# The first RMS root from the token rows of x, x loaded ahead of the modulation weights

## The reference

```python
mod = split(silu(c) @ ada_w + ada_b, 6)                  # six vectors of 1024 channels
h = x * rsqrt(mean(x * x, axis=-1) + 1e-6) * g_pre       # first root: one number per token
a = h * (1 + mod[1]) + mod[0]                            # a scale and a shift per channel
b_gate, c_gate, v = split(a @ sc_w_in, 3)
y = (b_gate * conv3(c_gate * v)) @ sc_w_out
x = x + mod[2] * rmsnorm(y, g_post)                      # its own norm follows: the second root of x
```

## Time and profile before

| | us |
|---|---|
| median of 3 runs | 1722.91 |
| lowest and highest run | 1722.45, 1723.51 |
| the profiled execution | 1723.58 |
| its span, first to last instruction | 1721.8 |
| PE busy in it | 1697.1 (99%) |
| DVE busy | 1096.6 (64%) |
| ACT busy | 699.0 (41%) |

### The profile page before, as it was taken

The page is one execution under the profiler, slowest core; times in us unless marked ns, Lnnn a source line. Parts: engine busy times, 40 slices in busy tenths (PEclk is TensorE's granted clock), DMA queues, the critical chain, the costliest instruction groups (busy, mean ns, idle before and its releaser), DMA issues.

```text
span 1721.8 us, 21514 instructions
## 1 busy us (share of the span) xinstructions
PE 1697.1 (99%) x7685; PEld 1374.9 (80%) x7685; DVE 1096.6 (64%) x1663; ACT 699.0 (41%) x1021; POOL 159.3 (9%) x145
## 2 busy tenths in 40 slices
PE   8999999999999999999999999999999999999999
PEld 7888868888888789788888888877656888888888
DVE  6799885353534685645663663669998666366364
ACT  4322353232323345844432432446676443243242
POOL 1000400000000040000000000005892000000000
PEclk9999999999999999999999999999999999999999
DMA  9576314323333132002222222232210323223222
GB/s 295 178 243 221 125 57 137 98 98 98 116 98 98 49 99 93 31 26 98 98 98 98 97 98 89 81 99 74 74 49 28 120 97 99 85 94 112 75 85 86
DMA packets 182338, 176.22 MB, mean 102 GB/s; under 512 B 3304, under 2 KB 181740, under 8 KB 182268
## 3 DMA queue, kind: packets, MB, share of 16 engines
q1 hardware_dynamic: 182268, 175.29, 31.8%
HBM read 173.15 MB, written 2.10 MB: 102 GB/s over the span
## 4 chain that ended last, share of the span: by engine, by line
PE 87%; DVE 5%; POOL 4%; issue 2%; ACT 1%; DMA 1%; POOLq 0%; SPq 0%; DVEq 0%; ACTq 0%
PE PSUM L1582 23%; PE PSUM L1583 23%; PE PSUM L1584 23%; POOL CP L537 3%; DVE PSUM L1514 1%; PE PSUM L1947 1%; PE PSUM L1945 1%; PE PSUM L1946 1%; PE PSUM L1920 1%; PE PSUM L1900 1%; PE PSUM L1672 1%; PE PSUM L1614 1%; PE PSUM L1616 1%; PE PSUM L1979 1%; PE PSUM L1980 1%
## 5 line engine op out<-in xcount | busy, mean ns | idle before, releaser
L577 ACT ACTIVATE WH<-RAW 128x1024 fp32r<-128x1024 f32 x274 | 281.5, 1052 | 726.6 <-PE PSUM L1584 684.5
L1582 PE MATMUL PSUM<-XH,WH 128*128 128x512 f32 x1152 | 449.5, 390 | 0.0
L1583 PE MATMUL PSUM<-XL,WH 128*128 128x512 f32 x1152 | 448.2, 389 | 0.0
L1584 PE MATMUL PSUM<-XH,WL 128*128 128x512 f32 x1152 | 448.2, 389 | 0.0
L977 DVE TENSOR_TENSOR WL<-RAW,WH 128x1024 fp32r<-128x1024 f32 x274 | 343.6, 1276 | 8.1 <-ACT WH L577 8.0
L1582 PEld LDWEIGHTS PSUM<-XH,WH 128*128 128x128 f32 x1152 | 216.3, 188 | 45.7 <-issue 0.7
L1583 PEld LDWEIGHTS PSUM<-XL,WH 128*128 128x128 f32 x1152 | 216.3, 188 | 45.4 <-issue 0.7
L1584 PEld LDWEIGHTS PSUM<-XH,WL 128*128 128x128 f32 x1152 | 216.3, 188 | 44.8
L1582 PE MATMUL PSUM<-HH,WH 128*128 128x512 f32 x644 | 251.3, 390 | 0.4
L1584 PE MATMUL PSUM<-HH,WL 128*128 128x512 f32 x644 | 250.6, 389 | 0.0
L1583 PE MATMUL PSUM<-HL,WH 128*128 128x512 f32 x644 | 250.6, 389 | 0.0
(11 more groups left out here) (347 smaller groups left out, 2000.7 us busy)
## 6 DMA issues: line engine op xcount, KB each, us to landing
RAW<-in_ffn_w_up SPq DMA_DIRECT2D x44, 1024.0 KB, 5.0
ARAW<-in_ada_w SPq DMA_DIRECT2D x24, 1024.0 KB, 5.3
RAW<-in_mlp_w_in SPq DMA_DIRECT2D x16, 1024.0 KB, 5.3
RAW<-in_mlp_w_out SPq DMA_DIRECT2D x16, 1024.0 KB, 4.9
RAW<-in_ffn_w_down SPq DMA_DIRECT2D x16, 1024.0 KB, 5.1
RAW<-in_sc_w_in SPq DMA_DIRECT2D x9, 1024.0 KB, 5.2
RAW<-in_even_w_in SPq DMA_DIRECT2D x8, 1024.0 KB, 5.6
RAW<-in_odd_w_pw SPq DMA_DIRECT2D x16, 512.0 KB, 4.7
```

The lines of the kernel that those rows point to most:

```text
L577: act.activation(WH[:, j, a:b, :], RAW[:, j, a:b, :], ACT.Copy).then_inc(s_hi, 1)
L1582: pe.matmul(o, wh, mh[:, k, :], start=(k == 0), stop=False)
L1583: pe.matmul(o, wh, ml[:, k, :], start=False, stop=False)
L1584: mm = pe.matmul(o, wl, mh[:, k, :], start=False, stop=(k == kn - 1))
```

## The change

x is loaded in four blocks of 128 tokens, ahead of all modulation weights. ACT squares each block of rows as it lands, with the sum over the channels accumulated per token, takes ln and exp of the 128x4 sums, and writes the roots on four diagonals of 128x128; PE multiplies these by ones, which puts the root of every token on all partitions in `ST_BANK`, where `scaled_x` reads it. The squares and additions of the chunks on ACT, POOL and DVE and their two sums on PE are gone. PE transposes block by block, DVE copies half a block at a time. The scale column of chunk 0 is made by PE alone (`first_scale`, 8 steps), so that `mod_unit(4, P)` covers chunk 1 alone. The shift column of chunk 0 has a semaphore of its own, and the four last shift steps of stage 0 come behind chunk 0's products of the first unit. DVE makes the columns of the chunks one by one; `mod_unit(5)` stands ahead of chunk 1's subtraction. On PE the fillers at the start are 16 rather than 26, the shift products of stage 1 and its scale columns are put elsewhere between the products. Since the bank now holds the root, ACT turns it back into the mean square (Ln, Exp with -2) before unit 12, and DVE's last addition for the second root multiplies by 1024.

```diff
-    return 8 * (stat - (stat > ST_X1))
+    return 8 * (stat - (stat > ST_X0) - (stat > ST_X1))
...
+        SCALE_BANK, SHIFT_BANK = 3, 6
...
                 a = (4 + i, i)[part]
                 if i == 1:
-                    sp.wait_ge(s_xt, DC)
-                elif i >= 2:
-                    sp.wait_ge((s_ad, s_ap)[part], i - 1)
+                    sp.wait_ge(s_xt, 2 * TB)
+                    sp.wait_ge(s_xq, TB)
+                elif i == 2:
+                    sp.wait_ge((s_ac, s_ap)[part], 1)
+                elif i == 3:
+                    sp.wait_ge((s_ad, s_ap)[part], 2)
...
+                                 ).then_inc(s_raw0[i] if i else s_raw00[u], 16)
...
+            for b in range(TB):
+                sp.dma_start(XROW[:, b, :], i["x"][0, b * P:b * P + P, :]).then_inc(s_xin[b], 16)
             load_first_mod(0, 0)
-            sp.dma_start(XROW[:, :, :], x_rows).then_inc(s_xin, 16)
             load_first_mod(0, 1)
...
-            for n, (a, b) in enumerate(((0, 1), (2, 3), (0, 2))):
-                if n < 2:
-                    pool.wait_ge(s_sqr, 2 * n + 2)
-                else:
-                    pool.wait_ge(s_sqg, 2)
-                pool.tensor_tensor(first_square(a), first_square(a), first_square(b), ALU.add).then_inc(s_sqg, 1)
...
-            def first_hi(i):
...
+            def first_hi(i, units=range(FIRST)):
...
+                for u in units:
...
-                    act.wait_ge(s_raw0[i], 16 * FIRST)
+                    if i == 0:
+                        act.wait_ge(s_raw00[u], 16)
+                    else:
+                        act.wait_ge(s_raw0[i], 16 * FIRST)
                     act.activation(hi, raw, ACT.Copy).then_inc(s_hi0, 1)
...
+            def root_of_rows():
+
+                for b in range(TB):
+                    act.wait_ge(s_xin[b], 16)
+                    act.activation(MACC[:, (2 + b) * D:(3 + b) * D], XROW[:, b, :], ACT.Square,
+                                   accum_out=sc_(S_RS + b)).then_inc(s_xq, 1)
+                act.wait_ge(s_const, 1)
+                act.wait_ge(s_xq, TB)
+                act.activation(sc_(S_RR, TB), sc_(S_RS, TB), ACT.Ln, bias=sc_(S_EPS), scale=1.0 / D).then_inc(s_ln, 1)
+                act.wait_ge(s_ln, ST_X0 + 1)
+                act.activation(sc_(S_RR, TB), sc_(S_RR, TB), ACT.Exp, scale=-0.5).then_inc(s_r, 1)
+                act.wait_ge(s_r, ST_X0 + 1)
+                act.wait_ge(s_const, 7)
+                for b in range(TB):
+                    act.activation(TF[:, 1, b * P:b * P + P], IDENT[:, :].bitcast(F32), ACT.Copy, scale=sc_(S_RR + b)
+                                   ).then_inc(s_dg, 1)
...
-            for c in range(DC):
-                act.wait_ge(s_xu, c + 1)
-                act.activation(first_square(c), X[:, c, :], ACT.Square).then_inc(s_sqr, 1)
-            first_hi(0)
-            act.wait_ge(s_const, 1)
-            rms(ST_X0, 1.0 / D)
-            for i in range(4):
+            root_of_rows()
+            first_hi(0, (0, 1))
+            act.wait_ge(s_sm, 3)
+            split_shift(0, S_GS0, S_MOD, (0,))
+            first_hi(0, (2,))
+            act.wait_ge(s_sm, 4)
+            split_shift(0, S_GS0, S_MOD, (1,))
+            first_hi(1)
+            for i in range(1, 4):
                 act.wait_ge(s_sm, 3 * i + 4)
                 split_shift(0, S_GS0, S_MOD, (2 * i, 2 * i + 1))
                 if i < 3:
...
+            act.activation(PS_[:, S0_BANK, :], PS_[:, S0_BANK, :], ACT.Ln).then_inc(s_ms, 1)
+            act.wait_ge(s_ms, 1)
+            act.activation(PS_[:, S0_BANK, :], PS_[:, S0_BANK, :], ACT.Exp, scale=-2.0).then_inc(s_ms, 1)
...
-            act.activation(SQ[:, :], TF[:, 0, :], ACT.Ln, bias=sc_(S_EPS), scale=1.0 / D).then_inc(s_ln, 1)
+            act.activation(SQ[:, :], TF[:, 0, :], ACT.Ln, scale=1.0 / D).then_inc(s_ln, 1)
...
-            def mod_unit(a):
+            def mod_unit(a, c0=0):
...
+                dst = MACC[:, a * UW + c0:a * UW + UW]
                 for k in range(8):
-                    w, s = src[:, k, :], sc_(S_CS + k)
+                    w, s = src[:, k, c0:UW], sc_(S_CS + k)
...
-                tt(TA[:, c % 2, :], X[:, c, :], R[:, :], ALU.mult).then_inc(sp_t, 1)
...
+                tt(TA[:, c % 2, :], X[:, c, :], PS_[:, ST_BANK, :], ALU.mult).then_inc(sp_t, 1)
+
+            def x_lo(c):
+
+                dve.wait_ge(sp_h, c + 1)
+                tt(XL[:, c, :], TF[:, c % 2, :], XH[:, c, :].bitcast(F32), ALU.subtract).then_inc(s_x, 1)
...
+            def copy_x(b):
+
+                for h in range(2):
+                    step = 2 * b + h
+                    dve.wait_ge(s_xt, step + 1)
+                    dve.tensor_copy(X[:, 4 * h:4 * h + 4, b * P:b * P + P],
+                                    PS_[:, step % 4, :].rearrange("p (c t) -> p c t", c=4)).then_inc(s_xu, 1)
...
             dve.wait_ge(s_cs, 1)
-            mod_unit(4)
-            for c in range(DC):
-                dve.wait_ge(s_xt, c + 1)
-                dve.tensor_copy(X[:, c, :], PS_[:, c % 4, :]).then_inc(s_xu, 1)
-            for n, (a, b) in enumerate(((4, 5), (6, 7), (4, 6))):
-                if n < 2:
-                    dve.wait_ge(s_sqr, b + 1)
-                else:
-                    dve.wait_ge(s_sq2, 2)
-                tt(first_square(a), first_square(a), first_square(b), ALU.add).then_inc(s_sq2, 1)
-            first_lo(0)
-            for i in range(4):
-                if i == 0:
-                    dve.wait_ge(s_r, ST_X0 + 1)
-                    scaled_x(0)
+            for b in range(TB):
+                copy_x(b)
+            mod_unit(4, P)
+            dve.wait_ge(s_xu, 8)
+            dve.wait_ge(s_ss, ST_X0 + 1)
+            scaled_x(0)
+            scaled_x(1)
+            dve.wait_ge(s_ac, 1)
+            for n in range(2):
+                gs = dve.tensor_scalar(sc_(S_GS0 + n), PS_[:, SCALE_BANK, 8 + n:9 + n], sc_(S_B1 + n), col("gains", n),
+                                       ALU.add, ALU.mult)
+            gs.then_inc(s_sm, 1)
+            first_lo(0, (0, 1))
+            dve.wait_ge(s_ap0, 1)
+            tt(sc_(S_MOD), PS_[:, COL_BANK, 0:1], col("ada_b", 0), ALU.add).then_inc(s_sm, 1)
+            x_lo(0)
+            first_lo(0, (2,))
+            dve.wait_ge(s_ap, 1)
+            tt(sc_(S_MOD + 1), PS_[:, SHIFT_BANK, 1:2], col("ada_b", 1), ALU.add).then_inc(s_sm, 1)
+            mod_unit(5)
+            x_lo(1)
+            scaled_x(2)
+            scaled_x(3)
+            first_lo(1)
+            for i in range(1, 4):
                 dve.wait_ge(s_ap, i + 1)
                 dve.wait_ge(s_ac, i + 1)
                 for n in (2 * i, 2 * i + 1):
                     dve.tensor_scalar(sc_(S_GS0 + n), PS_[:, COL_BANK, 8 + n:9 + n], sc_(S_B1 + n), col("gains", n),
                                       ALU.add, ALU.mult).then_inc(s_sm, 1)
                 tt(sc_(S_MOD + 2 * i, 2), PS_[:, COL_BANK, 2 * i:2 * i + 2], col("ada_b", 2 * i, 2), ALU.add).then_inc(s_sm, 1)
-                if i == 0:
-                    scaled_x(1)
-                for c in (2 * i, 2 * i + 1):
-                    dve.wait_ge(sp_h, c + 1)
-                    tt(XL[:, c, :], TF[:, c % 2, :], XH[:, c, :].bitcast(F32), ALU.subtract).then_inc(s_x, 1)
+                x_lo(2 * i)
+                x_lo(2 * i + 1)
...
-            tt(v, PS_[:, S0_BANK, :], v, ALU.add).then_inc(s_ss, 1)
+            dve.wait_ge(s_ms, 2)
+            stt(v, PS_[:, S0_BANK, :], float(D), v, ALU.mult, ALU.add).then_inc(s_ss, 1)
...
-                pe.wait_ge(s_sq2, 3 + p + 1)
+                pe.wait_ge(s_sq2, p + 1)
...
-                    mm = pe.matmul(PS_[:, COL_BANK, 2 * i + n:2 * i + n + 1], src[:, 1, k, n * P:n * P + P],
+                    bank = SHIFT_BANK if (i, n) == (0, 1) else COL_BANK
+                    mm = pe.matmul(PS_[:, bank, 2 * i + n:2 * i + n + 1], src[:, 1, k, n * P:n * P + P],
                                    sc_(S_CS + k), start=(k == 0), stop=(k == 7))
+                    if (i, step) == (0, 7):
+                        mm.then_inc(s_ap0, 1)
...
+            def first_scale(first, last):
+
+                if first == 0:
+                    pe.wait_ge(s_ar[0], 16)
+                    pe.wait_ge(s_cs, 1)
+                for k in range(first, last):
+                    pe.matmul(PS_[:, SCALE_BANK, 8:9], ARAW[:, 0, k, 0:P], sc_(S_CS + k), start=(k == 0), stop=(k == 7))
+
+            def first_root():
+
+                pe.wait_ge(s_dg, TB)
+                for b in range(TB):
+                    mm = pe.matmul(PS_[:, ST_BANK, b * P:b * P + P], ONES[:, :], TF[:, 1, b * P:b * P + P],
+                                   start=True, stop=True)
+                mm.then_inc(s_ss, 1)
...
-            def first_chunk_of_x():
+            def first_chunk_of_x(u):
...
-                for u in range(FIRST):
-                    pe.wait_ge(s_lo0, pieces(0, u))
-                    raw, hi, lo = first_unit(u, 0)
```

(129 more changed lines are left out.)

2 lines of the change are left out of this document (removed).

## The result

The changed kernel takes 1728.96 us, median of 9 runs, against 1723.45 for the kernel before beside it (9 runs): a ratio of 1.0044, 95% interval 1.0028 to 1.006. It is slower by 5.5 us, where 0.2 to 0.7 us less was forecast. The profiled execution took 1728.43, its span is 1726.7 (before 1721.8).

The account below looks back on a forecast made before the run. PE was taken as the bound, so only an earlier stage 1 helps: 3.6 us won at the start, 0.95 left, less 0.75 for clock and 0.06, gives 0.15 gained. Forecast 1722.7 us, range 1720.0 to 1725.0.

Parts of the forecast that it names:

- the new wait ahead of stage 1: PE waits about 1.5 us before stage 1, because one unit of products covers the 2.9 us chain from the scale columns.
- the sum: Step-by-step timing from load to stage 1: PE starts chunk 0 at 23.5 instead of 27.11, stage 1 at 39.1 instead of 40.05.
- the term for the clock: Half clock between 18 and 23.5 us may delay chunk 0; cost between 0 and 1.5 us, taken as 0.75.
- Rival B: Slower: half clock twice, at 18 to 23.5 us and the wait before stage 1; loss of 2 to 4, 1725.9; chance 0.08.
- The wait for the copies: PE goes on only behind DVE's last copy of x, put at about 14.8 us; no clock cost was charged.
- Rival A: The start's gain carries through with the clock held and chunk 2's chain covered: 3.4 to 3.8 us won, 1719.2; chance 0.12.
- the chain to chunk 2: From stage 1's scale columns over DVE, two ACT passes and DVE's subtraction: 2.9 us, ahead of stage 1.
- Rival C: Load blocks land together or weights are held back at the start; under 1 us, its chance within the forecast's 0.80.

Follow-up runs that it names:

- x2_fillers: Changed kernel with two more 128x512 fillers on PE ahead of chunk 0; median 1738.0 us, ratio 1.0083, two full-clock runs at 1721.88 and 1723.24.
- x1_regroup: Changed kernel with stage 1's 16 shift steps in four runs of four between products instead of two of eight; 1725.69 us, ratio 1.0025.
- x3_both: Changed kernel with the edits of x1_regroup and x2_fillers together; 1728.96 us, ratio 1.0032, six runs near 1723 and six at 1734 to 1735.
- z3_26_fillers: Changed kernel with 26 fillers at the start instead of 16, nothing else; 1735.92 us, ratio 1.0072.
- y1_gap: x3_both with eight 128x128 fillers in PE's wait for DVE's last copies of x; 1723.71 us, ratio 1.0004.
- y2_gap_alone: Changed kernel with only eight 128x128 fillers in PE's wait for DVE's last copies of x; 1727.85 us, ratio 1.0027.
- y3_sooner: y1_gap with stage 1's scale columns one unit sooner on PE, the last eight shift steps in one run before them; 1722.73 us, ratio 1.0002.
- y4_early: y3_sooner with 8 fillers at the start instead of 16; 1721.89 us, ratio 0.9995.

## Why the prediction was wrong

**Right, within 0.3 us each** (forecast, then the profile after): first copy of x 9.9, 10.14; copies' end 14.8, 15.02; the eight multiply-adds of 128 columns 2.95, 2.99 (14.94 to 17.93); the shift column's addition 21.7 to 21.9, 21.79; `XH` 23.4, 23.45; the new wait ahead of stage 1 about 1.5, 1.43. With the clock held (x2_fillers, one filler on the path at 0.94) stage 1 starts at 39.91, where the sum of 39.1 and 0.94 says 40.0. The order on the engines, and the durations taken from the rows, were sound. One figure on the way is not: the sum has the scale columns of stage 1 at 36.0, where its own terms (30.9 + 1.45 + 1.7 + 1.5) give 35.55. x2_fillers has them at 36.48, less its filler 35.54. The chain behind them is counted from 36.2, about where they end, so stage 1's start was little touched.

**The step that failed is the term for the clock**: "The cost lies between 0 and 1.5, I take 0.75." It was 5.95 us in the profiled execution, 45.05 against 39.1, nearly all of it in three parts. Up to chunk 1's first product, 33.74 against 30.9, 2.8: that is one stretch twice as long as the one before the change, which keeps its own filler busy longer, halves chunk 0, and thereby delays the shift column on which `mod_unit(5)` waits (29.09 against 26.1). Then 1.7 for the second run of steps (3.40 against 1.7) and 1.2 for the unit behind it (38.56 to 41.27 against 1.5); the 0.2 left lie in the products and scale columns beside them. The term had priced one fall, as in the earlier trace rows, and only its effect on one filler and the steps beside it.

**Rival B, half clock twice, came closest** and was given 0.08; its price of 2 to 4 us was too low. It was right about the first place. The second it put at the 1.5 us wait before stage 1, but the clock was back at 42.0, ahead of that wait (43.6 to 45.05); the second stretch began at about 35.2, with the second run of eight steps. The evidence against B was misread: "between 28 and 60 the same mixture of products and steps held the full clock". It was not the same mixture. The kernel before puts 12, 10 and 10 records of steps between groups of six products; the change puts 16:

```profile
29.17 1.39 PE L1672 MATMUL PSUM<-small,ARAW 128*128 128x1 f32 x12
31.88 1.17 PE L1672 MATMUL PSUM<-small,ARAW 128*128 128x1 f32 x10
34.38 1.17 PE L1672 MATMUL PSUM<-small,ARAW 128*128 128x1 f32 x10
```

By the profiles above this matters in a run that has already lost the clock once, and x1_regroup shows what it is worth there, some 3 us.

**The wait for the copies** was in the sum, as part of when PE goes on, and no clock was charged to it, because the kernel before has a wait of 1.4 us at about the same place and keeps its clock. Behind that one stand 32 transposes in a row. Behind the new one of 1.83 stand a filler, one-column steps and small products. It bears on the worst runs, four of nine at 1735. Those four were not profiled themselves; that they are the kind seen in x3_both and z3_26_fillers rests on their times and clocks, and on y1_gap and y2_gap_alone, where there are none.

Rival A did not happen as such, but y3_sooner and y4_early show what it would have needed: the chain to chunk 2 covered by two units, and earlier copies. Rival C is out: the blocks of x landed early enough for ACT's squares to start at 6.13 and end by 11.6, and PE waited for no load behind 16 us. ACT did, 3.69 us for the first pieces of sc_w_in until 17.25; that is 4.7 us ahead of its work on chunk 0, which waited for DVE, so it cost nothing. The Trainium skill, page "TensorE: Matmul & The Clock Gate", section "HAM oscillation — how this bites in real kernels", says that bursts of matmuls parted by waits start cold again and again. The prediction weighed this and then only half believed it. The kernel before supported it less than the prediction says: its fall at 24.28 comes 2.9 us behind the end of a wait of 0.75 us (at 21.41), with PE busy between. x3_both fits it, for there the clock fell right behind a wait of 1.82 us. The second stretch of the changed kernel does not: ahead of it PE had waited no longer than 0.23 us since 15.16.

What stays open is where the clock falls in a given run: the same kernel, x2_fillers or x3_both, gives runs at 1.0 and at 0.991 with nothing changed. The runs point to the places that make the bad outcomes possible, not to what picks one. Half clock was also seen in the profiles of several changed kernels near 230 us (the second root; in the changed kernel itself a short stretch) and near 1200, and not in the profile of the kernel before. That profile is a run at 0.999; about a third of its runs had 0.997, and none of them was profiled. No experiment tried these places; in the changed kernel they cost nothing that can be seen, 5.0 us of delay at stage 1 against 4.9 in the span.

## What to carry to other kernels

The way to the first product may get shorter and the kernel slower, if PE fills it with waits and one-column matmuls: after any change at the start, read the granted clock of the stretch and that of every run, not PE's busy share. Price a fall of the clock by everything that is queued behind it, and the worst case as well as the likely one. Small matmuls put into time that PE would wait anyway cost nothing that showed here, and the runs 10 us above the others were missing with them; spreading one-column steps in shorter groups between large products is as cheap. With runs this uneven, compare whole sets of runs and their clocks, since one profile shows only one kind.

## What the runs showed of the hardware

- One-column steps in float32, 128x128 weights: 16 records take 1.84 us at full clock and 3.40 at half. At half the clock they took 1.85 times as long, although each moves a single column.
- Half clock held for 20 us while PE was busy throughout: in x3_both from about 16 to 36.5 us, with one-column steps and fillers of 128x512 in it.
- Time went with the granted clock of the run: in y1_gap eleven runs at 0.999 and 1.0 lie within 1.9 us, in x2_fillers seven runs from 1.0 to 0.988 spread over 17.
- In the changed kernel ACT's accumulation over a row brings a second instruction, ACTIVATION_READ_ACCUMULATOR of 0.18 to 0.19 us, behind each square of 128x1024 of 1.06 us.
